# Experts of a mixture layer in units of 512 columns, with each expert's sums, gather and give-back inside the steps of the next

## What is computed

```python
logits = (hf @ w_router).astype(jnp.float32)
top_val, top_idx = lax.top_k(logits, TOP_K)
gates = jax.nn.softmax(top_val, axis=-1)
...
def expert_block(args):
    xb, e = args
    return (jax.nn.silu(xb @ w_gate[e]) * (xb @ w_up[e])) @ w_down[e]
...
out = jnp.einsum('tk,tkd->td', gates.astype(y.dtype), y)
```

## Time and profile before

| | |
|---|---|
| time, median of 3 runs | 2652.91 us (2651.89 to 2653.14) |
| the profiled execution's own time | 2653.62 us |
| its span in the profile | 2651.7 us |
| PE busy | 2433.5 us (92%) |
| DVE busy | 1814.2 us (68%) |
| ACT busy | 1494.8 us (56%) |
| HBM read | 587.22 MB |
| stage with the nine passes | 629.6 to 1824.7 us |

### The profile page before, as it was taken

One profiled execution on the slowest core, in us unless ns is written; L12 is line 12 of the kernel. 1 busy time (PEld: TensorE's weight loads), 2 busy tenths in 40 slices (PEclk: granted clock), 3 DMA queues, 4 the chain that ended last, 5 costly groups with the idle time before them and its releaser, 6 DMA issues.

```text
span 2651.7 us, 31059 instructions
## 1 busy us (share of the span) xinstructions
PE 2433.5 (92%) x11217; PEld 1982.8 (75%) x11217; DVE 1814.2 (68%) x1837; ACT 1494.8 (56%) x1680; POOL 61.6 (2%) x96
## 2 busy tenths in 40 slices
PE   7888998977999999999999999897988998989997
PEld 6676887756878787878787878785777876777885
DVE  5675545676878787878787878687755455554454
ACT  4622444354767676767676767575664445455344
POOL 0000000004000000000000000000000000000000
PEclk9999999998999999999999999998999998999998
DMA  7203456307999899989899989796412553413541
GB/s 286 95 5 128 159 190 222 127 6 256 367 305 367 301 367 307 366 300 366 299 366 310 366 297 367 262 367 204 146 35 96 191 198 135 158 37 127 189 168 56
DMA packets 397135, 589.62 MB, mean 222 GB/s; under 512 B 12433, under 2 KB 301425, under 8 KB 396784
## 3 DMA queue, kind: packets, MB, share of 16 engines
q1 hardware_dynamic: 394432, 579.39, 63.4%
q0 software_dynamic: 2608, 8.93, 1.0%
HBM read 587.22 MB, written 1.05 MB: 222 GB/s over the span
## 4 chain that ended last, share of the span: by engine, by line
PE 75%; DVE 11%; ACT 7%; DMA 5%; issue 2%; DVEq 0%; SPq 0%; ACTq 0%
PE up L1814 15%; PE up L1815 14%; PE up L1816 14%; PE acc L1814 7%; PE acc L1816 7%; PE acc L1815 7%; DMA raw<-in_ffn_w 4%; DVE wl L1230 3%; ACT wh L757 3%; PE up L2191 2%; PE tp L2098 1%; ACT wh L960 1%; DVE wl L1544 1%; PE up L2003 1%; PE tp L1805 1%
## 5 line engine op out<-in xcount | busy, mean ns | idle before, releaser
L1544 DVE TENSOR_TENSOR wl<-raw,wh 128x2048 fp32r<-128x2048 f32 x378 | 864.9, 2292 | 129.4 <-ACT wh L960 117.2
L1814 PE MATMUL up<-wh,xTh 128*128 128x512 f32 x1888 | 760.1, 403 | 42.3 <-DVE wl L1544 15.0
L960 ACT ACTIVATE wh<-raw 128x2048 fp32r<-128x2048 f32 x378 | 723.3, 1918 | 60.9 <-PE acc L1816 57.0
L1815 PE MATMUL up<-wl,xTh 128*128 128x512 f32 x1888 | 742.7, 393 | 0.0
L1816 PE MATMUL up<-wh,xTl 128*128 128x512 f32 x1888 | 741.8, 393 | 0.0
L1230 DVE TENSOR_TENSOR wl<-raw,wh 128x2048 fp32r<-128x2048 f32 x171 | 389.3, 2291 | 388.3 <-ACT wh L757 387.5
L757 ACT ACTIVATE wh<-raw 128x2048 fp32r<-128x2048 f32 x171 | 324.4, 1916 | 390.8 <-PE up L1816 217.6
L1814 PEld LDWEIGHTS up<-wh,xTh 128*128 128x128 f32 x1888 | 358.9, 190 | 124.7 <-DVE wl L1230 19.5
L1816 PEld LDWEIGHTS up<-wh,xTl 128*128 128x128 f32 x1888 | 358.1, 190 | 77.0
L1815 PEld LDWEIGHTS up<-wl,xTh 128*128 128x128 f32 x1888 | 359.2, 190 | 68.9
L1814 PE MATMUL acc<-wh,hTh 128*128 128x512 f32 x864 | 342.3, 396 | 21.0 <-DVE hTl L1570 18.1
(11 more groups left out here) (333 smaller groups left out, 2031.8 us busy)
## 6 DMA issues: line engine op xcount, KB each, us to landing
raw<-in_moe_w_gate SPq DMA_DIRECT2D x252, 512.0 KB, 6.4
raw<-in_moe_w_up SPq DMA_DIRECT2D x252, 512.0 KB, 7.7
raw<-in_moe_w_down SPq DMA_DIRECT2D x126, 1024.0 KB, 7.8
raw<-in_ffn_w SPq DMA_DIRECT2D x32, 2048.0 KB, 9.0
raw<-in_hg_w_in SPq DMA_DIRECT2D x7, 2048.0 KB, 13.2
raw<-in_da_w_in SPq DMA_DIRECT2D x6, 2048.0 KB, 8.1
raw<-in_ffn_w_gate SPq DMA_DIRECT2D x11, 1024.0 KB, 7.0
raw<-in_ffn_w_up SPq DMA_DIRECT2D x11, 1024.0 KB, 11.0
```

The lines of the kernel that those rows point to most:

```text
L960: f(wh[:, x % SPLITS, :], raw[:, x % RAW, :], ACT.Copy).then_inc(m["hi"], 1)
L1544: V.tensor_tensor(wl[:, x % SPLITS, :], raw[:, x % RAW, :], wh[:, x % SPLITS, :].bitcast(F32), ALU.subtract).then_inc(m["lo"], 1)
L1814: mm(out, x_hi, w_hi, start=start, stop=False)
L1815: mm(out, x_hi, w_lo, start=False, stop=False)
```

## The change

A pass now has 7 units of 512 hidden columns (`EU = D_FFE // W`), each with two halves of gate, two of up and two of down, still 42 halves. Gate goes to bank `up[:, 0]`, up to `up[:, 1]`. The buffers `half`, `stage`, `tp[:, 0]` and `hTh/hTl` have one place of 512 columns each. A step t of PE is: gate products of unit t, transposes of unit t-1, up products of unit t, down products of unit t-1. At t = 7 the gate and up products are those of the next pass's first unit.

What stood between passes is spread over the steps of the next or the same pass: the copy of the down sums, now scaled by the gate weight of each token (`gs`) and split into `yeh` and `yel` (step 1), the give-back products with the 0/1 matrix `pickT` in split form (steps 2 and 3, eight products), the adds to `y` (steps 3 and 4), the transposes of `pick` and the sum for `gs` (step 4), the choice and the gather of the next pass (step 5, into `acc[:, 2:4]`), `xTh/xTl` of the gathered tokens (step 6). The extra passes run in the same chain, ahead of the last one. SP issues one transfer of 1 MB a half, with rows of 2 KB for gate and up, 4 KB for down. The first two halves of down in a pass are issued in reverse order, under one wait. The copy of `h` to `y` (ACT) moves behind the first splits.

```diff
-    EU = D_FFE // HALF
+    EU = D_FFE // W
-    for u in range(1, EU):
-        HALVES += [(G, u, 0), (G, u, 1), (DN, u - 1, 0)]
+    FIRST, PASS = 4, 6 * EU
+    half_no = lambda t, p: FIRST + 6 * (t - 1) + p if t else p
...
 SP
-            for x, (kind, u, part) in enumerate(HALVES):
...
+        def load_down(at, t_, p, w, u):
+            for part in (1, 0) if u == 0 else (0, 1):
+                load_half(at, t_, p + part, w, u * W + part * HALF, slice(0, D), 2, waits=u > 0 or part == 1)
...
 ACT
+        def expert_out(at):
+            act.wait_ge(moe["down"], at(EU, EU))
+            f(yeh, acc[:, 0:2, :].rearrange("p a (k n) -> p (a k) n", n=P), ACT.Copy, scale=gs[:, 0:1]).then_inc(moe["yeh"], 1)
+            for t_ in range(1, EU + 1):
+                if t_ < EU or following is not None:
+                    split_half(at, t_, 2)
+                    if t_ == 1 and before is not None:
+                        expert_out(before)
+                    split_half(at, t_, 3)
+                turned_hidden(at, t_)
+                down = 4 if t_ < EU or following is not None else 0
+                split_half(at, t_, down)
+                if t_ < EU or following is not None:
+                    gate_act(at, t_)
+                if t_ == 5:
+                    act.wait_ge(moe["turned"], at(1, 1))
+                    f(pickT, tp[:, 1, 0:2 * P], ACT.Copy)
+                    f(gs[:, :], tp[:, 1, 2 * P:2 * P + 1], ACT.Copy).then_inc(moe["pickT"], 1)
+                split_half(at, t_, down + 1)
...
 DVE
+            for t_ in range(1, EU + 1):
+                adds = before is not None and t_ in (3, 4)
...
+                turned_hidden(at, t_)
+                down = 4 if t_ < EU or following is not None else 0
+                split_half(at, t_, down)
+                split_half(at, t_, down + 1)
+                if t_ == EU - 1 and following is not None:
+                    for q in range(2):
+                        gathered(following, q)
+                        split_half(at, t_ + 1, q)
+                    gate_times_up(at, t_)
...
 PE
-            pe.wait_ge(m["ye"], i + 2)
-            pe.wait_ge(m["giveT"], i + 1)
-            for n in range(4):
-                mm(give_banks[n], giveT[:, n // 2, :], ye[:, (n % 2) * W:(n % 2 + 1) * W],
-                   start=True, stop=True).then_inc(m["give"], 1)
+            for t_ in range(1, EU + 1):
+                if t_ < EU or following is not None:
+                    gate_products(at, t_, following if t_ == EU else None)
+                turn_hidden(at, t_)
+                if t_ < EU or following is not None:
+                    up_products(at, t_)
+                down_products(at, t_, 4 if t_ < EU or following is not None else 0, before)
+                if t_ in (2, 3) and before is not None:
+                    if t_ == 3:
+                        pe.wait_ge(moe["added"], before(4, 6))
+                    give_back(before, t_ - 2, give_banks[0:2])
+                if t_ == 4:
+                    turn_choice(at)
+                if t_ == 5 and following is not None:
+                    if before is not None:
+                        pe.wait_ge(moe["added"], before(4, 8))
+                    gather(following)
```

More of the change, by code:

```diff
@@ L349, in _program, with counter, at, wait_count @@
     c_after = pl.chunk
-    G, DN = 0, 1
-    HALVES = [(G, 0, 0), (G, 0, 1)]
-    for u in range(1, EU):
-        HALVES += [(G, u, 0), (G, u, 1), (DN, u - 1, 0)]
[L355 to L366, removed]
+    FIRST, PASS = 4, 6 * EU
+    LAST = NE - 1
+    assert PASS % RAW == 0 and PASS % SPLITS == 0
+    def counter(reg, first):
+        def at(per, plus):
+            n = first * per + plus
+            return n if isinstance(reg, int) else reg * per + n
+        return at
+    half_no = lambda t, p: FIRST + 6 * (t - 1) + p if t else p
+    def wait_count(eng, s, n):
+        if not isinstance(n, int) or n > 0:
+            eng.wait_ge(s, n)
     T_cv = pl.take_turns(4)
@@ L448, in _program @@
     s_rl, s_rp, s_ra, s_rd = sem("router_logits"), sem("router_places"), sem("router_act"), sem("router_done")
[L449 to L452, removed]
+    moe = {n: sem(f"moe_{n}") for n in ("picked", "gath", "xgh", "xg", "turned", "pickT", "gate", "up", "act", "st", "T", "Th", "Te",
+                                      "hi", "lo", "used", "down", "yeh", "yel", "give", "added")}
+    m_ready = [sem(f"moe_ready{r}") for r in range(RAW)]
     cv_dw, cv_n = sem("conv_done"), sem("conv_normed")
@@ L558, in _, with weight @@
             cols_chunk(c_dao + i, t["da_w_out"], i * W)
[L560 to L572 removed]
+        def weight(name, e):
+            return t[name][0, bass.ds(e, 1), :, :].rearrange("a k n -> (a k) n")
@@ L1608, in _ @@
+        final = counter(n_extra, LAST)
+        expert(final, counter(n_extra, LAST - 1), None, None)
+        expert_out(final)
+        for n in range(4):
+            add(final, n, give_banks[n])
+        dve.wait_ge(moe["added"], final(4, 8))
         last_split = len(pl.halves)
@@ new lines, in up_products, with turn_hidden, down_products @@
+        def up_products(at, t_):
+            for part in range(2):
+                gate_up(at, t_, 1, part).then_inc(moe["up" if part else "used"], 1)
+        def turn_hidden(at, t_):
+            pe.wait_ge(moe["st"], at(EU, t_))
+            wait_count(pe, moe["Te"], at(EU, t_ - 1))
+            for k in range(4):
+                ins = nc.tensor.transpose(tp[:, 0, k * P:(k + 1) * P], stage[:, 0, k * P:(k + 1) * P], ident)
+            ins.then_inc(moe["T"], 1)
+        def down_products(at, t_, p, before):
+            pe.wait_ge(moe["Te"], at(EU, t_))
+            if t_ == 1 and before is not None:
+                pe.wait_ge(moe["yel"], before(1, 1))
+            for part in range(2):
+                w_hi, w_lo = split_ready(at, t_, p + part, 2)
+                for n in range(2):
+                    for k in range(2):
+                        kk = 2 * part + k
+                        t_k, c_ = slice(kk * P, (kk + 1) * P), slice(n * W, (n + 1) * W)
+                        ins = split_product(acc[:, n, :], hTh[:, 0, t_k], hTl[:, 0, t_k], w_hi[:, k, c_], w_lo[:, k, c_],
+                                            t_ == 1 and kk == 0, t_ == EU and kk == 3)
+                ins.then_inc(moe["down" if part else "used"], 1)
```

374 lines of the change are left out of this document (188 added, 186 removed).

## The result

The changed kernel takes **2590.98 us** (median of 4 runs, 2589.41 to 2596.35), the kernel before 2653.02 us on the same chip (4 runs, 2651.89 to 2653.19): a ratio of 0.9771, interval 0.9754 to 0.9788. That is 62 us less. 2593 were forecast. The profiled execution took 2589.41 us by its own time, its span is 2587.3 us.

A forecast was written before the change was run, and what follows sets the result against it. PE bounds the kernel, with 13.9 of each 131.9 us pass at its ends. Start, steps, border work, tail and branches put the last add at 1764.6 instead of 1824.65: 60 us less, 2593 us, range 2584 to 2622.

The forecast's parts named there:

- The border: Between passes: PE's period falls from 131.9 to 124.2 us, 7.7 us less a border.
- the step: Steady part: a step of 512 columns takes PE 16.86 us, twice a unit of before; each 0.1 us is 6 us.
- its 13.9 us: Part of each 131.9 us pass at its ends: waits of first and last units, gather, give-back, adds and xTl.
- The slack: First down half in each step: ACT and DVE chain 5.4 us, cover 5.9 us, so 0.5 us is left.
- rival 1: Every step: uncounted handshakes use up the thin slack, 0.1 to 0.5 us late each; 2618 at 0.4; chance 0.08.
- rival 2: Weight transfers bind at 339 GB/s, so a pass cannot go below 129.9 us; about 2630; chance 0.05.
- rival 3: Loop of single buffers: a late stage delays transposes, hTh and Silu, lengthening each step; slower than before, 2696; chance 0.05.
- the sum: From 650.8: 62 steps 1045.3, last step 8.3, gathers 28.6, give-backs 14.5, turns 7.2; ends at 1754.7.
- the turns: Turn of pick and sum for gs on PE: 0.8 us each, bounded by 0.4 and 1.2; nine are 7.2.
- the branches: Each engine reads n_extra and branches in mid-chain: 4 us taken, bounded by 0 and 6.
- The end: Last step, only down: transposes, open wait for hTh/hTl (2.0 and 0.5) and 5.4 us of products, 8.3 us.
- the tail: After the last step, open: ACT's copy 1.2, yel 1.3, first products 0.7, four adds 2.7: 5.9 us.

The follow-up runs named there:

- e1_give_end: The changed kernel with the copy of the sums, give-backs and adds put back at the end of their own pass: 2640.12 us.
- e4_slack_1024: The changed kernel with two more, unneeded copies of 128x512 on ACT behind hTh in every step: 2637.46 us.
- e6_rows_1k: The changed kernel with each gate or up half loaded by two 512 KB transfers with 1 KB rows instead of one of 1 MB: 2594.07 us.
- e5_stage_late: The changed kernel with DVE's product of Silu and up (stage) behind the next gate's two splits instead of ahead of them: 2592.90 us.
- e7_ends: The changed kernel with splits moved ahead of waiting work at the stage's start and in its very last step: 2583.45 us.
- e2_gather_late: The changed kernel with the gather one step later, at the end of step 6, just ahead of the gate products needing it: 2631.33 us.
- e9_both_late: The changed kernel with the give-back at its own pass's end and the gather at the end of step 6: 2671.89 us.

## Why the prediction was right

**The border, 7.7 us forecast.** It measures 131.9 - 123.7 = 8.2. The gather and the give-back kept their price (3.6 and 1.8 us). The rest of the pass, 123.7 - 7 x 16.80 - 3.6 - 1.8, leaves 0.7 for the turn of `pick` and the sum for `gs`; 0.8 were taken. The 0.5 more comes from the step: 16.78 to 16.81, not 16.86.

Where the 8.2 us went can be added up from rows of before. The open waits at 1.67, 2.00, 0.78 and 0.24 cost PE some 5.1 us a border, the distance to the next start counted as in e1_give_end. The give-back was 3.4 us and is 1.8. The seven steps give 0.4. And 0.8 to 0.9 are products at the low clock level, which the prediction did not see as a part of its 13.9 us (the last section shows them). That makes 8.0. That the placing is the cause is shown by experiment: putting back the give-back costs 49.6 us, the gather 41.9, both 77.9, more than the 61.2 us by which the stage became shorter. The split form of the give-back was not tried by itself; its 1.6 us are read from rows.

**The slack, 0.5 us forecast.** The row for it in the changed kernel, ACT, DVE and PE in one step:

```profile
953.75 0.60 ACT L983 ACTIVATE hTh<-tp 128x512 fp32r<-128x512 f32 x1 [1.24 <-PE tp L2194]
954.25 1.91 ACT L973 ACTIVATE wh<-raw 128x2048 fp32r<-128x2048 f32 x1
...
956.19 4.59 DVE L1573 TENSOR_TENSOR wl<-raw,wh 128x2048 fp32r<-128x2048 f32 x2 [0.15 <-ACT wh L973]
...
959.01 0.39 PE L1875 MATMUL acc<-wh,hTh 128*128 128x512 f32 x1
```

The first `wl` of down is ready at 956.19 + 2.3 = 958.5 and PE wants it at 959.01. The handshake of 0.15 that rival 1 feared to see three or four times occurs once. e4_slack_1024 measured the same margin from the other side. So rival 1 was ruled out by tenths: it would have begun with half a microsecond more on ACT.

**Transfers and single buffers (rivals 2 and 3).** e6_rows_1k and e5_stage_late put a price on each, none for rows of 1 KB and none for two splits more ahead of `stage`. In 1086 us the core took 353 GB/s without PE waiting for one transfer, 4% above the 339 at a share of 1.00 on which rival 2 was built. The Trainium skill ("Perfetto Trace Analysis", section "Roofline") says that a core that is alone may go beyond the 358 GB/s, up to about 120% of it; the slices of the profile reach 379 GB/s, so this trace agrees as far as it goes.

**Terms that were off, and cancelled in part.**
- From the first product of step 1 to the last step's transposes 1740.79 - 648.24 = 1092.6 us passed; the sum has 1099.6. Some 3.7 of the 7 is the step of 16.80, 0.9 the turns, and 4 the branches with the read of `n_extra`: PE shows no time for them. Against these stand 1.6 us of slow products behind the first pause (those that e7_ends takes away), which the sum does not have. The 2.6 us of the earlier trace rows on which the 4 were built were DVE's: 1.46 of idle time in which it reads and branches, then the choice. PE waited for that in the kernel before. Now DVE reads inside a step, at 1513 us, and the gathers on both sides of it (1476.66 and 1600.31) are 123.65 us apart, as the others are. DVE's row in the kernel before:

```profile
1688.96 0.48 DVE L1553 TENSOR_SCALAR arena<-cst,slot 128x128 f32<-128x128 f32 x2 [1.46 <-issue]
```

- The end was mis-sized: 8.3 us for transposes, wait and products were 13.4 (1740.79 to 1754.2), and the tail 6.4 instead of 5.9. The 2.5 us for "an open wait for `hTh/hTl` as in rows 4" did not look at what stands behind `hTh` on ACT: there are the last two splits, so a wait of 4.81, and behind it ten products at the low clock. e7_ends shows that the order is the reason: the wait is then 1.49.
- From the gather to step 1 I had 21.2 us, 21.4 were measured. That the stage began 2.8 us earlier is no effect of the change.

Together: -2.8 ahead of the stage, +0.2 at its start, -7.0 in the steps, +5.6 at the end and tail, -0.4 behind it are -4.4, from a span of 2591.7 us by the forecast (2651.7 less 60) to the measured 2587.3. The mechanism of the forecast is right. That it came within 2 us of the median is in part luck: the branches were 4 us too much, the steps 3.7, the end 5.6 too little and the slow products 1.6, with opposite signs, and the stage began 2.8 us earlier for no reason in the forecast. A change of the size of these terms would have been missed by that sum.

## What to carry to other kernels

Work at the border of two loops costs what PE stands open for, even if each piece is one microsecond; placed inside the next iteration, behind a reserve that a timeline shows, it cost nothing here; the larger tiles that came with it gave 0.06 us a step. Add up the smallest slack of a step from rows before placing anything there, and price an open wait at 0.15 to 0.3 us over what its row will show (0.27 in e4_slack_1024), more if products behind it fall to the low clock. At a loop's last iteration, look at what stands in order behind the instruction that waits: splits of weights that had been there for 6 us waited with it.

## What the runs showed of the hardware

PE's products fell to the low clock level (0.43 us apart, twice the 0.23) behind pauses of 2.0 to 4.8 us, though not behind each. In e2_gather_late the same 3.03 us pause was followed by slow products in one pass and by none in another. In e9_both_late a pause of 3.02 us was followed by none in seven passes of eight, while the pauses of 2.8 and 0.8 or 0.9 us, 20 us behind it, were in all eight. In the stages here it was mostly five to thirteen slow products each time, 1.0 to 2.8 us.

Shorter pauses were not safe from it. The kernel before waits 2.0 us (2.1 once) at the last unit of each of its nine passes. In five of them the clock fell within 1.5 us or so of that wait, in four it stayed. One of each, the wait from the timeline of PE and then the stretches with the granted clock, as in rows 5; the wait of the second is the first row:

```profile
886.02 0.50 PE L1814 MATMUL acc<-wh,hTh 128*128 128x512 f32 x1 [2.00 <-DVE hTl L1570]
...
886.00:891.00 5.00, 4.98 (x17) 4.08 (x18) 5.00 (x6) 2.56 (x3) 0.00 (x0) 0.66 1.10 336
1018.00:1023.00 5.00, 4.41 (x26) 3.92 (x27) 5.00 (x8) 3.96 (x4) 0.00 (x0) 1.00 1.14 337
```

Of its six passes from the second gather to the eighth, the two without slow products there take 131.1 and 131.2 us, the four with them 132.1 to 132.5. In the changed kernel PE has no pause at the borders, and no slow product either from 652 to 1746 us. What exactly decides whether the clock falls behind a pause stays open.
